# Latent attention in a two-layer trunk: where the softmax rows are divided, one PSUM bank for a head pair, and which engine subtracts the high parts

## The reference, cut to what matters

```python
for blk in range(S // ATTN_BLOCK):            # 4 blocks of 128 queries
    s = (einsum('bqhd,bkhd->bhqk', q_n[:, q0:k_end], k_n[:, :k_end])
         + einsum('bqhr,bkr->bhqk', q_r[:, q0:k_end], k_r[:, :k_end])) * scale
    s = where(k_idx[None, :] <= q_idx[:, None], s, -inf)
    p = softmax(s, axis=-1)
    outs.append(einsum('bhqk,bkhd->bqhd', p, v[:, :k_end]))
o = concatenate(outs, axis=1).reshape(B, S, 16 * 64)
return o @ w_o
```

## Time and profile before

| what | us |
|---|---|
| median of 3 runs | 1305.01 (1304.06 to 1309.29) |
| span of the profiled execution, first to last instruction | 1303.4 |
| TensorE busy | 1227.1 (94%) |
| VectorE busy | 686.6 (53%) |
| ScalarE busy | 454.7 (35%) |
| GpSimd busy | 292.2 (22%) |
| mean granted TensorE clock | 0.981 |

### The profile page before, as it was taken

One profiled execution on the slowest core, in us unless ns is written; L12 is line 12 of the kernel. 1 busy time (PEld: TensorE's weight loads), 2 busy tenths in 40 slices (PEclk: granted clock), 3 DMA queues, 4 the chain that ended last, 5 costly groups with the idle time before them and its releaser, 6 DMA issues.

```text
span 1303.4 us, 15832 instructions
## 1 busy us (share of the span) xinstructions
PE 1227.1 (94%) x5829; PEld 1012.0 (78%) x5829; DVE 686.6 (53%) x955; ACT 454.7 (35%) x725; POOL 292.2 (22%) x255
## 2 busy tenths in 40 slices
PE   6888999899999999999997999889999999999997
PEld 4667777678888888888876997666888888888885
DVE  5867888734534434334479434795443343343432
ACT  4336666543212212222342324763322221221242
POOL 4222222222201102002134103562220020110211
PEclk8999999999999999999999999899999999999998
DMA  4201011222232332322222322011323223233211
GB/s 151 67 22 27 23 26 32 87 77 85 97 108 87 106 96 88 105 89 97 89 75 65 125 86 73 25 49 34 100 94 100 95 97 99 94 98 96 97 65 64
DMA packets 113887, 104.00 MB, mean 80 GB/s; under 512 B 20934, under 2 KB 112164, under 8 KB 113836
## 3 DMA queue, kind: packets, MB, share of 16 engines
q1 hardware_dynamic: 113344, 102.98, 25.2%
q10 hardware_dynamic: 492, 0.31, 0.1%
HBM read 101.17 MB, written 2.11 MB: 79 GB/s over the span
## 4 chain that ended last, share of the span: by engine, by line
PE 76%; DVE 11%; issue 6%; ACT 3%; POOL 3%; DMA 0%; ACTq 0%; DVEq 0%; POOLq 0%
PE ps L1473 23%; PE ps L1475 23%; PE ps L1474 23%; DVE nmax L1113 2%; POOL xl L570 1%; DVE xl L972 1%; DVE yc L1290 1%; DVE qtmp L1105 1%; DVE diag L987 1%; POOL wlo L513 1%; ACT whi L638 1%; ACT prob L714 1%; ACT uh L728 1%; DVE rinv L1118 1%; DVE yc L1287 1%
## 5 line engine op out<-in xcount | busy, mean ns | idle before, releaser
L1473 PE MATMUL ps<-xl,whi 128*128 128x512 f32 (+1 forms) x688 | 270.7, 394 | 5.3 <-DVE krot L1052 3.2
L638 ACT CAST whi<-raw 128x2048 fp32r<-128x2048 f32 (+4 forms) x150 | 184.7, 1259 | 247.9 <-PE ps L1475 239.5
L1475 PE MATMUL ps<-xh,wlo 128*128 128x512 f32 (+1 forms) x688 | 268.6, 390 | 0.0
L1474 PE MATMUL ps<-xh,whi 128*128 128x512 f32 (+1 forms) x688 | 268.6, 390 | 0.0
L967 DVE TENSOR_TENSOR wlo<-raw,whi 128x2048 fp32r<-128x2048 f32 (+2 forms) x86 | 187.5, 2184 | 151.9 <-ACT whi L638 151.9
L1473 PE MATMUL ps<-ul,whi 128*128 128x512 f32 x608 | 237.3, 390 | 1.2 <-POOL wlo L513 1.2
L1475 PE MATMUL ps<-uh,wlo 128*128 128x512 f32 x608 | 236.7, 389 | 0.0
L1474 PE MATMUL ps<-uh,whi 128*128 128x512 f32 x608 | 236.6, 389 | 0.0
L543 POOL TENSOR_TENSOR ul<-sq,uh 128x512 fp32r<-128x512 f32 x64 | 83.6, 1308 | 521.2 <-ACT uh L817 521.2
L1195 DVE TENSOR_TENSOR h<-ps,h 128x512 f32<-128x512 f32 x80 | 55.0, 689 | 197.4 <-PE ps L1475 192.5
L1473 PEld LDWEIGHTS ps<-xl,whi 128*128 128x128 f32 (+1 forms) x688 | 129.0, 188 | 35.1 <-issue 4.9
(11 more groups left out here) (234 smaller groups left out, 1653.1 us busy)
## 6 DMA issues: line engine op xcount, KB each, us to landing
raw<-in_mlp_w SPq DMA_DIRECT2D x64, 1024.0 KB, 5.2
raw<-in_mlstm_w_in SPq DMA_DIRECT2D x12, 1024.0 KB, 5.4
raw<-in_mla_w_o SPq DMA_DIRECT2D x4, 1024.0 KB, 5.0
raw<-in_mlstm_w_o SPq DMA_DIRECT2D x4, 1024.0 KB, 5.4
raw<-in_mla_w_in SPq DMA_DIRECT2D x3, 1024.0 KB, 5.6
raw<-in_mla_w_uq SPq DMA_DIRECT2D x16, 192.0 KB, 2.5
x_tok<-in_x SPq DMA_DIRECT2D x4, 512.0 KB, 5.9
mb<-m_rows SPq DMA_DIRECT2D x8, 256.0 KB, 3.2
```

What stands on the lines that cost most here:

```text
L638: last = sc.copy(hi, src)
L1473: mm(o, ah, bl, start=first, stop=False)
L1474: mm(o, ah, bh, start=False, stop=False)
L1475: ins = mm(o, al, bh, start=False, stop=last)
```

## The change

- The probabilities are no longer multiplied by the reciprocals of their row sums. Unnormalised exponentials are transposed and multiplied by v, and the result, which has the queries along its columns, is multiplied by the reciprocals at the end. For this the reciprocals of both heads (8 columns, high and low parts: 16) are transposed on TensorE (`turn_scales`), copied by ScalarE (`rows_turned`), spread to 128 rows by four products with a 0/1 matrix `pick` (`spread_scales`), copied by ScalarE (`rows_spread`) and applied by VectorE (`o_scaled`).
- `vh` and `vl` get a gap of zeros between the two heads' columns, so that each head's products are zero on the other head's rows, and both heads add into one bank. The other bank holds the scales. One `o_high` and one `o_low` a pair, on 128 rows, take the place of two on 64.
- `q_low` and `o_low` are on GpSimd. On ScalarE `q_high` of the second head stands ahead of the strip's split.
- After the last pair tile pair `T_WO + 2` is started before step 7 of tile pair `T_WO`, with its last step behind it; strips 2 and 3 follow as before.
- VectorE's and TensorE's hardware loops start at pair 2, with pair 1 written out.

The core of the diff:

```diff
@@ gpsimd
+            for t in (vh, vl):
+                g.memset(gap_of(t).bitcast(F32), 0.0)
+            g.tensor_tensor(pick[:, :, :].rearrange("r b (e n) -> r b e n", e=2), spot[0], spot[1], ALU.add)
...
+            def attention(p, first=False, last=False):
+                q_low(p, 1)
+                if not last:
+                    strip_low(N_PAIR + 2, "kq", p)
+                else:
+                    strip_low(N_WO, "full")
+                v_low(p)
+                if not first:
+                    o_low(p - 1)
+                if not last:
+                    q_low(p, 2)
+                    strip_low(N_PAIR + 3, "q", p)
 
             pool.wait_ge(wlo_ready, N_PAIR)
             strip_low(N_PAIR, "kq")
+            q_low(0, 0)
             strip_low(N_PAIR + 1, "q")
...
             strip_low(N_WO + 1, "full")
+            o_low(PAIRS - 1)
@@ scalar
                 pt_high(i, 0, 0)
                 exp(i, 0, 2)
+                q_high(1, i, 1)
                 if last:
                     split(N_WO, "half 0")
                 else:
                     split(N_PAIR + 2, "kq", i, 2, 48)
                 pt_high(i, 0, 1)
-                q_high(1, i, 1)
                 exp(i, 0, 3)
+                if not first:
+                    rows_turned(i)
...
                 exp(i, 1, 0)
+                v_high(i, first)
                 if not first:
-                    o_high(i, -1)
-                sc.copy(vh[:, :, :], v_slot(i)).then_inc(v_hi, 1)
+                    rows_spread(i)
...
                 exp(i, 1, 2)
+                if not first:
+                    o_high(i)
                 if not last:
                     q_high(0, i, 2)
...
+            rows_turned(PAIRS)
             split(N_WO + 1)
-            o_high(PAIRS, -1)
+            rows_spread(PAIRS)
+            o_high(PAIRS)
@@ vector
+            def attention(i, first=False, last=False, second=False):
                 row_max(i, 0, 2)
                 pt_low(i, 0, 0)
-                normalise(i, 0, 2)
                 q_table(i, 1)
                 row_max(i, 0, 3)
                 pt_low(i, 0, 1)
-                q_low(i, 1)
-                normalise(i, 0, 3)
...
+                row_max(i, 1, 2)
                 if not first:
-                    o_low(i, -1)
+                    o_scaled(i, second)
                 pt_low(i, 1, 0)
                 if not last:
                     q_table(i, 2)
@@ tensor
-                pe.wait_ge(p_norm, i * 8 + (s + 1))
+                pe.wait_ge(s_exp, i * 8 + (s + 1))
...
                 if not first:
+                    turn_scales(i, second)
                     weigh(i, -1)
                 turn_p(i, 0, 2)
+                if not first:
+                    spread_scales(i)
                 scores(i, 1, 0)
...
+            turn_scales(PAIRS)
             weigh(PAIRS, -1)
+            side_by_side(N_WO + 1, T_WO + 2, range(0, 4), lambda k: None)
+            spread_scales(PAIRS)
+            side_by_side(N_WO + 1, T_WO + 2, range(4, KD - 1), lambda k: None)
             out_products(range(KD - 1, KD))
-            strips(N_WO, T_WO, range(1, 4), uh, ul)
+            side_by_side(N_WO + 1, T_WO + 2, range(KD - 1, KD), lambda k: None)
+            strips(N_WO, T_WO, range(2, 4), uh, ul)
```

More of the change, by code:

```diff
@@ L1162, in attention @@
                     k_low(0, i, 1)
-                normalise(i, 1, 1)
                 row_max(i, 1, 2)
+                if not first:
+                    o_scaled(i, second)
                 pt_low(i, 1, 0)
@@ L1178, in attention @@
                 if not last:
-                    normalise(i, 2, 0)
                     row_max(i, 2, 1)
+                row_scales(i)
                 pt_low(i, 1, 3)
-                o_low(i, 0)
             attention(0, first=True)
-            with dve.Fori(1, PAIRS - 1) as i:
-                own.enter(i, 1, 8)
+            attention(1, second=True)
+            with dve.Fori(2, PAIRS - 1) as i:
+                own.enter(i, 2, 3)
                 attention(i)
-                own.leave(1, PAIRS - 1)
+                own.leave(2, PAIRS - 1)
             attention(PAIRS - 1, last=True)
-            o_low(PAIRS, -1)
+            o_scaled(PAIRS)
             dve.wait_ge(wlo_ready, N_WO + 2)
@@ L1623, in weigh @@
                         pe.wait_ge(v_hi, i + (lead // 2 + 1))
-                    mm(ps[:, B_PV + e, P * j:S], vh[:, j, :], pth[e][:, j, P * j:S], start=(j == 0), stop=False)
+                        if e == 0 and not first:
+                            pe.wait_ge(o_new, i)
+                    mm(o_all[:, P * j:S], vh[:, j, cols], pth[e][:, j, P * j:S], start=(e + j == 0), stop=False)
                 for j in range(TT) if 1 in steps else ():
-                    o = ps[:, B_PV + e, P * j:S]
+                    o = o_all[:, P * j:S]
                     if j == 0:
@@ L1629, in weigh @@
                         pe.wait_ge(t_lo, i * 8 + (4 * lead + 4))
-                    mm(o, vl[:, j, :], pth[e][:, j, P * j:S], start=False, stop=False)
-                    last = mm(o, vh[:, j, :], ptl[e][:, j, P * j:S], start=False, stop=(j == TT - 1))
-                if 1 in steps:
+                    mm(o, vl[:, j, cols], pth[e][:, j, P * j:S], start=False, stop=False)
+                    last = mm(o, vh[:, j, cols], ptl[e][:, j, P * j:S], start=False, stop=(e == 1 and j == TT - 1))
+                if e == 1 and 1 in steps:
                     last.then_inc(pv_mm, 1)
+            def turn_scales(i, first=False):
+                pe.wait_ge(r_inv, i)
+                if not first:
+                    pe.wait_ge(r_ready, i - 1)
+                tr(ps[0:16, B_R, 0:P], rinv2[:].bitcast(F32), ident[:]).then_inc(rt_mm, 1)
+            def spread_scales(i):
+                pe.wait_ge(rt_ready, i)
+                for b in range(TT):
+                    last = mm(ps[:, B_R, P * b:P * b + P], pick[:, b, :], rt[:], start=True, stop=True)
+                last.then_inc(r_mm, 1)
             strip_ready(N_VA)
@@ L1661, in _, with attention @@
             q_half(0, (N_PAIR + 1) % 2)
-            def attention(i, first=False, last=False):
+            def attention(i, first=False, last=False, second=False):
                 turn_p(i, 0, 0, first)
@@ L1729, in out_products @@
             def out_products(ks):
-                side_by_side(N_WO, T_WO, ks, lambda k: pe.wait_ge(o_lo, 2 * k + 2))
+                side_by_side(N_WO, T_WO, ks, lambda k: pe.wait_ge(o_lo, k + 1))
             attention(0, first=True)
-            with pe.Fori(1, PAIRS - 1) as i:
+            attention(1, second=True)
+            with pe.Fori(2, PAIRS - 1) as i:
                 attention(i)
```

105 lines of the change are left out of this document (57 added, 48 removed).

## The result

The changed kernel is slower: 1323.18 us, the median of 4 runs (1322.42 to 1324.23), against 1306.9 for the kernel before on the same chip (4 runs, 1304.06 to 1309.29). The ratio is 1.0134, with a 95% interval of 1.0117 to 1.0151. Forecast were 1319.8 in a range of 1307 to 1328, and slower with 0.80. The profiled execution has a span of 1322.4 us, 19.0 more than that of before. The kernel before is itself uneven: of its 37 runs beside the experiments 24 took 1303.8 to 1306.9 us and 13 took 1308.5 to 1309.7 us, these at a mean granted clock of 0.973 to 0.976, the others at 0.976 to 0.984.

What follows compares the result with a forecast made beforehand. TensorE, busy 94% of the span, was taken as the bound. +3.8 us up to the end of attention and +11.0 there made +14.8 on a span of 1303.4: 1318.2, with the median 1.6 above, 1319.8; range 1307 to 1328.

Steps and rivals of the forecast that it cites:

- The pairs: Steady head pairs in attention: each 0.43 us longer in spite of VectorE's relief, pairs 1 to 6 together +2.6 us.
- the strip's 2.70 us: GpSimd's weight-strip subtraction in a pair's first half: taken as 2.70 us after q's, so the k product starts at 7.75.
- The spread of the scales: First half of a pair: row-scale copy behind an exponential delays the spread to about 6.0 us, still before the k product.
- the second half: Second half of a pair: third score product can go at 5.6 us against 5.73 before; -0.15 us taken.
- The first pair: Start of attention: q product +0.9 us, k product +1.8, less 0.15 behind it; together +2.5 us.
- The last pair: Last head pair: TensorE still waits for GpSimd's strip, but output products start at 250.9 instead of 252.16; -1.3 us.
- The end: End of attention: TensorE waits 5.2 us for GpSimd's strip, then 5.3 us for strip 2; +11.0 us with clock loss.
- the clock behind them: Lower granted TensorE clock after the two waits at the end of attention: priced at 1.6 us each.
- B: Rival for the attention stage: VectorE's queue binds it, so waits vanish; pairs of 18.5 us, total 1298; chance 0.12.
- C: Rival for the end of attention: it costs nothing, as a strip comes early or ScalarE overtakes; 1309 us; chance 0.13.
- D: Rival for the pairs: ScalarE or a blocked VectorE row-scale copy delays exponentials; pairs of 22 us, total 1329; chance 0.12.
- VectorE's reads of PSUM: VectorE in the pairs: nothing large staying there is blocked by GpSimd; if wrong, the sum would be 16 us higher.

Runs made afterwards that it cites:

- e4: Changed kernel with q's subtraction back on VectorE and ScalarE's copy of the second head's q back behind the strip's split; 1310.57 us, ratio 1.0035.
- e8: Changed kernel with q's subtraction back on VectorE, ScalarE's q copy still ahead of the strip's split; 1319.32 us, ratio 1.0086.
- e9: Changed kernel with only ScalarE's copy of the second head's q back behind the split, q still subtracted on GpSimd; 1325.69 us, ratio 1.0143.
- after_again: The changed kernel run a second time, nothing altered; 1324.3 us, ratio 1.013 to the kernel before.
- e1: Changed kernel with TensorE's old tile order at the end of attention, everything else as changed; 1317.31 us, ratio 1.0087.
- e2: Changed kernel with ScalarE copying strip 1 of the projection earlier, inside the last pair; 1318.43 us, ratio 1.0087.
- e3: Changed kernel with strip 1 copied early in the last pair and tile pair 0 closed with five steps of pair 1 still to come; 1309.4 us, ratio 1.0021.
- e6: Kernel before with only the new tile order at the end of attention; 1318.88 us, ratio 1.010.
- e7: Kernel before with only q's low part on GpSimd and ScalarE's copy of the second head's q ahead of the split; 1322.33 us, ratio 1.013.
- e10: Kernel before with strip 2's first tile computed once more than needed, 24 added products in front of strip 2; 1314.43 us, ratio 1.0058.

## Why the prediction was right, and where its sizes were off

**The pairs.** The mechanism is shown: VectorE's relief, 6 us a pair, gives nothing while q's and the strip's subtractions stand in one queue (20.70 us), and 4.2 us of relief give 1.5 us when they don't (e4). e8 and e9 show that the engine and ScalarE's order each suffice to lose most or all of that. The size was off by 0.46 us in pair 3, +0.43 predicted and -0.03 measured, and by 3.0 in the sum: pairs 1 to 6 gave -0.4 us in place of +2.6 (their seven starts lie 124.54 us apart from first to last before, 124.12 after). The term is the strip's 2.70 us from the earlier trace rows: the same four pieces took 2.24, and the k product came after 7.39 us, not 7.75. The 2.70 held a collision that the change itself takes away. In the kernel before, VectorE's subtraction of q runs beside the strip, and the strip's third piece takes 0.78 us; with q on GpSimd it takes 0.31. First before, then after:

```profile
161.81 1.23 DVE L972 TENSOR_TENSOR xl<-qtmp,xh 128x512 fp32r<-128x512 f32 x1
162.44 0.78 POOL L513 TENSOR_TENSOR wlo<-raw,whi 128x64 fp32r<-128x64 f32 x1
...
165.60 0.31 POOL L533 TENSOR_TENSOR wlo<-raw,whi 128x64 fp32r<-128x64 f32 x1
```

The strip took 2.72 in e4 and 2.69 in e8, which have q on VectorE, and 2.24 in e9, which has it on GpSimd; its first piece took 0.72 to 0.74 in all of them, so the idle time before it makes no difference. The spread of the scales came at 5.92 us, as worked out (6.0), and so did the second half: 5.63 us to the third score product against 5.6, though the half gained 0.26 and not 0.15.

**The first pair.** +2.5 predicted. The first transpose moved by 0.55 (0.9 predicted), the k product came 8.08 us behind it (7.75 predicted, 5.98 before), and pair 1 started 2.76 us later. The first of these is no clean measure, since it holds the load ahead of the stage: that transpose starts at 95.12 here and at 96.56 in `after_again`. From it to pair 1 the changed kernel takes 2.2 us more (2.5 in `after_again`), where 1.65 was worked out.

**The last pair.** Its output products start 11.33 us after its first transpose, 12.84 before: -1.51, predicted -1.3. TensorE still waits for GpSimd's strip there, 2.50 us. Between these products and the last value product the changed kernel takes 0.62 us more, which I had not priced. Of these, 0.48 lie in the first twelve output products (4.45 us against 3.97). Behind the wait of 2.50 us the granted clock is 0.50 from 254 to 257, where the prediction left the clock out. In all the stage stood at +1.45 at its last value product and not at +3.8.

**The end.** Both waits came where they were put, for the strips that were named, and at nearly the predicted length: 4.85 against 5.2, 5.34 against 5.3. e1, e2, e3 and e6 take each away, or bring it into the kernel before. Mis-sized is the clock behind them. The 15 products behind the first wait took 6.37 us where they would take 3.41 at full clock, 2.96 lost; the 12 behind the second took 5.18 for 2.73, 2.45 lost. I had taken 1.6 for each from the earlier trace rows, where the wait was 3.82 us and the slow row 3.3 us long; behind these waits the slow rows are 6.1 and 5.2 us long. It is not a fixed price: in `after_again`, behind waits of 4.86 and 5.34 us, 1.55 and 1.7 us were lost, which is what I had taken. The whole end came to 12.5 - 1.45 = 11.1 up to strip 2 and 2.5 behind it, 13.6 in all, where 11.0 was predicted.

**The sum.** +1.45 + 13.6 = 15.0 against +14.8: the sum agrees closely since the stage up to the last value product was priced 2.4 too high and the end 2.6 too low. That is luck in part. The rest of the measured 19.0 is the untouched layer, which the prediction didn't have at all. By the medians on the same chip the difference is 16.3 us, by the ratio 17.5.

**The rivals.** B wanted pairs of 18.5 us with a k product before 6.6. The changed kernel has neither; e4 has 19.18 and 6.60, so even with free queues 0.7 us of B's gain isn't there: TensorE's wait for q's low part stays, 4.5 us over eight pairs. C fell by the two waits; e3 shows what it would have been worth. D would have shown as pairs of 22 us. The blocked VectorE copy that D feared does occur in e2 and e3, in the last pair, where it takes 3.1 us in place of 0.17, but TensorE doesn't wait for it. That VectorE's reads of PSUM are not held beside GpSimd rested on the table product of the earlier trace rows, which overlaps the strip for 0.17 us only. A better row is the subtraction of a 128x256 block out of PSUM at 161.48 in the kernel before: 0.41 us inside the strip, and 0.42 at 172.93, where GpSimd is idle. Of the smaller things: GpSimd's 8.9 busy us a pair stand for 9.5 predicted, and VectorE kept 65% of its busy time in a pair where I wrote near half.

## What to carry to other kernels

Moving work to an idler engine helps only if it isn't queued there ahead of something that the bound engine waits for; look at when the input comes, not at the engine's busy share (GpSimd was idle for 6 us, and still late). When tiles are reordered to hide a latency, follow both chains: is the tile's operand there at the new place, and which buffer is freed later because the other tile now closes later. A duration read from the kernel before can hold a collision that the change removes, as the strip's 2.70 us did. And a wait can cost more than its length: here waits of about 5 us cost 1.6 to 3.0 us more in clock.

## What the hardware showed that I had not expected

- The slow stretches differ in length: 3.3 us behind 3.82 us, 5.2 behind 5.34, 6.1 behind 4.85, all at a granted 0.50 to 0.52, but 3.1 behind 4.86 in `after_again`. The wait's length alone doesn't say it.
- Nor does it say whether the clock falls. In e7 the same wait of 1.93 or 1.94 us was followed by a lower clock in four of six pairs (0.57 over 3.3 us in pair 3) and by 1.00 in the other two (pair 2). In e8 a wait of 0.45 us was followed by 0.68 once, while the steady pairs with waits of 0.2 to 1.2 us in the changed kernel ran at 1.00 throughout.
- GpSimd's subtraction can be held by VectorE's. A 128x64 piece of the strip took 0.78 us across VectorE's subtraction of q and 0.31 without it.
- The other way round it can be long for a tiny instruction: in e3 VectorE's copy of 8 columns of reciprocals took 3.09 us, beside a GpSimd subtraction of 4.61 us that ended just before it. In the changed kernel the same copy took 0.17.

```profile
265.91 3.09 DVE L1184 CAST rinv<-rinv 128x8 fp32r<-128x8 f32 x1
```

- VectorE's q subtraction, with both inputs in SBUF, took 0.68 us while GpSimd was idle (the kernel before, at 172.33) and 1.26 beside GpSimd's strip (e4, its next pair at 176.50, in the strip's 175.48 to 178.21). By the Trainium skill, SBUF — State Buffer, "Who interferes with whom", an operation of VectorE with two SBUF inputs contends with a GpSimd instruction that reads SBUF, which agrees. It was not held for the strip's whole 2.7 us. That the strip's cut into four pieces is the reason fits the rows (the piece that was running when it began ended at 177.20, the subtraction at 177.75) but wasn't tested.
- The granted clock of a layer that was not changed lay between 0.86 and 0.94 in the profiled executions, with some 5 us in it (the changed kernel, e10). At this kernel's length that is 0.4%, and it is as large as several terms of the sum.
